# A hybrid attention and gMLP block on one core: the attention's short matmuls issued in two places of a product

## The reference, cut to what matters

```python
h = rms_norm(x, pre_norm)
q, k, v, gate_a, u_b, v_b, gate_b, mg_a, mg_b = split(h @ w_in)
o_a = sliding_window_attention(q, k, v, sinks, rel_bias)   # 16 query heads, 2 kv heads, window 128
y_a = (o_a * silu(gate_a)) @ w_branch_a
o_b = spatial_gating(gelu(u_b), gelu(v_b), ...)
y_b = (o_b * silu(gate_b)) @ w_branch_b
out = (sigmoid(mg_a) * y_a + sigmoid(mg_b) * y_b) @ w_out
x = x + rms_norm(out, post_norm)
```

## Time and profile before

| | |
|---|---|
| median of 3 runs | 908.33 us (908.08 to 909.26) |
| the profiled execution | 907.86 us, its span 906.1 us |
| granted clock of TensorE, mean | 0.998 |
| PE busy | 898.7 us, 99% of the span |
| DVE busy | 640.1 us, 71% |
| ACT busy | 491.0 us, 54% |
| POOL busy | 499.4 us, 55% |

### The profile page before, as it was taken

How to read it: one execution, slowest core, us unless ns; L and a number is a source line. 1 busy time by engine, 2 the same in 40 slices (tenths; PEclk the granted TensorE clock), 3 DMA queues, 4 the chain that set the end, 5 groups by cost and what they waited for, 6 DMA issues and landing times.

```text
span 906.1 us, 12649 instructions
## 1 busy us (share of the span) xinstructions
PE 898.7 (99%) x4332; PEld 754.0 (83%) x4332; DVE 640.1 (71%) x1135; ACT 491.0 (54%) x948; POOL 499.4 (55%) x395
## 2 busy tenths in 40 slices
PE   9999999999999999999999999999999999999997
PEld 7888888888888888888888888888888888888886
DVE  6766794655656564656565678688689878989968
ACT  6554355766756675757566664344444434534563
POOL 4565235777686868695868685445542252043236
PEclk9999999999999999999999999999999999999999
DMA  8889764422222253323222243533188550435004
GB/s 307 195 200 247 243 204 106 136 77 90 71 91 85 82 139 129 94 77 98 72 84 91 82 150 95 187 122 122 59 303 323 186 209 1 139 116 210 1 1 186
DMA packets 126591, 122.50 MB, mean 135 GB/s; under 512 B 23208, under 2 KB 95936, under 8 KB 126272
## 3 DMA queue, kind: packets, MB, share of 16 engines
q1 hardware_dynamic: 124288, 118.27, 41.2%
q10 hardware_dynamic: 2240, 3.43, 1.2%
HBM read 89.68 MB, written 35.15 MB: 138 GB/s over the span
## 4 chain that ended last, share of the span: by engine, by line
PE 98%; ACT 0%; DVE 0%; POOL 0%; issue 0%; DVEq 0%; POOLq 0%; ACTq 0%
PE acc L970 51%; PE acc L1150 11%; PE acc L823 9%; PE ps_m L1150 7%; PE ps_t L1150 7%; PE ps_t L987 3%; PE ps_m L1017 3%; PE acc L913 2%; PE ps_t L997 2%; PE ps_t L853 1%; PE ps_m L853 0%; PE acc L1042 0%; PE ps_t L839 0%; PE ps_t L855 0%; PE ps_m L855 0%
## 5 line engine op out<-in xcount | busy, mean ns | idle before, releaser
L970 PE MATMUL acc<-mv,w_hi 128*128 128x512 f32 x1344 | 353.1, 392 | 0.0
L970 PEld LDWEIGHTS acc<-mv,w_hi 128*128 128x128 f32 x1344 | 245.0, 188 | 45.0
L970 PE MATMUL acc<-mv,w_lo 128*128 128x512 f32 x672 | 181.1, 391 | 0.0
L970 PEld LDWEIGHTS acc<-mv,w_lo 128*128 128x128 f32 x672 | 126.2, 188 | 28.3
L1751 POOL TENSOR_TENSOR w_lo<-sums,w_hi 128x1024 fp32r<-128x1024 f32 x48 | 116.0, 2418 | 46.4 <-ACT w_hi L1316 38.4
L1751 POOL TENSOR_TENSOR w_lo<-raw,w_hi 128x1024 fp32r<-128x1024 f32 (+1 forms) x48 | 95.7, 1994 | 41.5 <-ACT w_hi L1309 35.9
L1150 PE MATMUL acc<-right,left 128*128 128x512 f32 x432 | 98.7, 389 | 0.0
L1150 PEld LDWEIGHTS acc<-right,left 128*128 128x128 f32 x432 | 81.0, 188 | 17.2 <-DVE left L2131 0.4
L1796 POOL TENSOR_SCALAR_AFFINE_SELECT pt_prev<-pt_pack 128x512 fp32r<-128x512 f32 x64 | 41.7, 652 | 85.7 <-DVE pt_pack L2067 85.7
L1518 ACT ACTIVATE prob<-neg_s,neg_max 128x129 f32<-128x129 f32 x128 | 50.6, 397 | 68.6 <-DVE neg_max L2076 68.5
L823 PE MATMUL acc<-mv 128*128 128x512 f32 x288 | 69.3, 394 | 0.6 <-ACT mv L1183 0.6
(11 more groups left out here) (282 smaller groups left out, 1680.8 us busy)
## 6 DMA issues: line engine op xcount, KB each, us to landing
raw<-in_w_in SPq DMA_DIRECT2D x56, 512.0 KB, 4.0
ht_d<-sums SPq DMA_DIRECT2D x8, 512.0 KB, 5.1
mix_d<-mix_b SPq DMA_DIRECT2D x8, 512.0 KB, 3.9
ga_d<-gate SPq DMA_DIRECT2D x16, 256.0 KB, 2.0
tb<-tb_d SPq DMA_DIRECT2D x4, 1024.0 KB, 5.2
ub<-mix_d SPq DMA_DIRECT2D x7, 512.0 KB, 3.5
gb_d<-ub SPq DMA_DIRECT2D x7, 512.0 KB, 2.6
x_both<-in_x SPq DMA_DIRECT2D x6, 512.0 KB, 6.3
```

Source lines behind the costliest of these rows:

```text
L970: ins = nc.tensor.matmul(bank, (w_lo if y == 2 else w_hi)[:, left + k * P:left + (k + 1) * P], right[:, (OPW if y == 1 else 0) + k * HALF: ...
```

## The change

In a product with attention work, transposes and scores come behind the third long matmul, and values behind the ninth. Nothing is added or removed; the order on PE's queue is the only thing that differs, and the other engines' queues are as before.

```diff
-            def attend(p, k):
+            def attend_values(p, k):
                 if 5 <= k < 13:
                     values(p, k - 5)
+
+            def attend_scores(p, k):
                 if 3 <= k < 11:
                     transpose_p(p, k - 3)
                 if k < 8:
...
             def product(n, x, at=None):
                 product_waits(n, x)
                 if at:
-                    product_mms(n, x, 0, 6)
-                    attend(*at)
-                    product_mms(n, x, 6, 12).then_inc(prod, 1)
+                    product_mms(n, x, 0, 3)
+                    attend_scores(*at)
+                    product_mms(n, x, 3, 9)
+                    attend_values(*at)
+                    product_mms(n, x, 9, 12).then_inc(prod, 1)
                 else:
```

## The result

| | before | after |
|---|---|---|
| median | 908.36 us (908.08 to 909.26) | 937.62 us (936.61 to 938.1) |
| span of the profiled execution | 906.1 us | 934.9 us |
| PE busy | 898.7 us, 99% | 907.3 us, 97% |

The ratio is 1.0317, with a 95% interval of 1.0305 to 1.0329: 29.3 us slower, where 25.2 were forecast. The profiled executions lie 28.8 us apart.

A forecast was written before the change was run, and what follows sets the result against it. PE's queue, 99% busy and without waits in the attention, was taken to set the end. Losses of 0.13 + 0.62 + 0.65 + 1.75 = 3.15 us a head pair, times 8 = 25.2, gave a median of 933.5 us, range 919 to 942.

The forecast's parts named there:

- Short matmuls at their usual cost, split at 0: On PE, short matmuls last the same behind short or long ones, so splitting the group in two costs 0.
- the rival "faster": On PE, a second short group behind a long matmul saves 0.05 in 48 steps: 2.4 us, 905.9; chance 0.03.
- Step 5, 0.13: PE's scores in step 5 of a head pair wait for DVE's evaluation of step 4's scores: 0.13 us lost.
- Steps 6 and 7, 0.62 and 0.65: Scores wait for DVE's evaluation, queued behind the pack that waits for values: 0.62 and 0.65 us lost per head pair.
- Step 9, 1.75: Transposes in step 9 wait for step 8's pack, delayed by a chain from step 7's evaluation: 1.75 us per head pair.
- The surcharge of 0.15: Extra cost of the transposes' wait in step 9, taken as the middle between 0.04 and 0.26 us.
- Steps 8 and 10 clear: Transposes in steps 8 and 10 come after the pack they need, with margins of 0.3 us: no loss.
- Eight head pairs alike: Head pair 6 stands for all eight: 3.15 us for a head pair, times 8 = 25.2.
- PE's busy time: In the changed profile, PE's busy time stays within a few microseconds and its idle time grows by 25.
- The rival that put 27 us on the clock: A pause of 1.75 us drops PE from 2.4 to 1.2 GHz for one step: 27 us more, 961; chance 0.03.
- the one in which more follows: POOL's masks and ACT's evictions make a product wait too: up to 1.5 us a pair more, 945; chance 0.06.
- the first rival: Give in the chain hides step 9's loss, only steps 5 to 7 lose: 11.2 us, 919.5; chance 0.10.

The follow-up runs named there:

- experiment 1: Changed kernel with the two groups swapped: values behind the third long matmul, transposes and scores behind the ninth; 909.13 us, ratio to before 1.001.
- experiment 4: Changed kernel with DVE's first two additions of a head pair moved from the end of step 7 to the end of step 8, behind the pack; 922.84 us.
- experiment 8: Changed kernel with values behind the twelfth long matmul, so nine long matmuls between scores and values, not six; 957.75 us, ratio to before 1.053.
- distance 0: Changed kernel with one group behind the sixth long matmul, values last: no long matmuls between scores and values (the distance); 915.23 us, ratio to before 1.0057.
- experiment 3: Changed kernel, PE's order kept, with DVE's evaluation of the scores ahead of the pack of the same step; 909.63 us, ratio to before 1.0021.

## Why the prediction was right

The mechanism, its places and the sign came out as forecast, and the time within 4.1 us. The terms that came out short are small and of one kind, what a signal or a start after a wait costs, but for a delay in one head pair; 0.6 us of the difference stands outside the attention.

*What bounds the kernel.* PE without waits meant that an order can hardly gain. No order tried here is faster than the kernel before, whose order has no wait to remove.

*Short matmuls at their usual cost, split at 0.* Right: experiment 1, which does not show the gain of the rival "faster" either. Transposes and scores still take 0.69 together behind a long matmul, as this row and the next long matmul of the changed kernel show.

```profile
478.03 0.38 PE L997 MATMUL ps_t<-ident,prob 128*128 128x128 f32 x2
...
478.72 1.32 PE L970 MATMUL acc<-mv,w_hi 128*128 128x512 f32 x5
```

The rule weighed against it (the Trainium skill, TensorE: Matmul & The Clock Gate, Back-to-back issue gap, about 81 ns for a 128-column matmul in a stream) does not describe these transposes, at 0.11 in either kernel.

*Step 5, 0.13.* Measured 0.14. The margin of 0.17 less the values' 0.24 was the right reading.

*Steps 6 and 7, 0.62 and 0.65.* Measured 0.74 and 0.72. The term that was mis-sized is the signal from the values to the pack. I took 0.04, the distance from transposes to pack; it is 0.11 (487.52 to 487.63). It applies to both steps. The surcharge of 0.06 on the scores was a little short too: from 489.51 to 489.57 is 0.06, but the second score matmul then follows at 0.22 instead of 0.20.

*Step 9, 1.75.* Measured 1.81. The chain from the evaluation of step 7 to the pack of step 8 is as stiff as assumed, and experiment 4 shows that it is this chain. The surcharge of 0.15 was a middle between two bounds, as no row showed it; by luck it is the distance at which a waiting transpose starts behind the pack (503.13 to 503.28); the second transpose then follows at 0.14 instead of 0.11, which is half of what was short.

*Steps 8 and 10 clear.* Right, with 0.03 and 0.00, and experiment 8 shows how little was left.

*Eight head pairs alike.* Not quite: head pair 4 loses 0.37 more in step 7. The prediction took one head pair for all. In pair 4 the pack of step 6 starts 0.46 behind the values' end instead of 0.11, and the scores of step 7 pay for it. The kernel before already has this pack 0.24 behind the transposes' end instead of 0.04, without loss there. What holds this pack back is open.

*The clock.* The granted clock stayed at 1.00 in the attention part, 2.4 GHz, through eight pauses of 1.6 us and sixteen of 0.5 or less.

```profile
161.00:565.00 404.00, 383.87 (x1945) 317.43 (x1944) 222.11 (x666) 247.01 (x638) 277.38 (x227) 1.00 0.28 88
```

That is the row by stage of 161 to 565 us; the 1.00 is the clock.

*PE's busy time.* This sign was off: it was to stay within a few microseconds and the idle time to grow by 25. Busy time grew by 8.6 and idle time by 20.2 (7.4 to 27.6), since the end of the matmul ahead of each pause, which in a full stream lies under the next matmul, now counts by itself.

The rival that put 27 us on the clock did not come about, nor did the one in which more follows; and the tail of step 9, which the first rival had hidden, was paid in full.

## What to carry to other kernels

Before moving work on the busiest engine, look for waits on its progress on other engines that are met long before they count, and ask what moves them behind their deadline. The price of such a wait is not its length but what stands behind it in its queue: with the same wait of the pack, 28 us became 1.1 us when the evaluation of the scores went ahead of it on DVE. Size it as a margin, from the releaser's end to the need, step by step; here that gave each step within 0.12 us, but for one step of one head pair. Read the margin of every repetition, and take off what a start after a wait costs.

## What the runs showed that was not expected

The loss bends upward with the distance. A head pair loses 0.6 at distance 0, 1.4 at 3, 3.4 at 6 and 6.1 at 9 (sums of the rows above). Once a step waits, it grows by about 0.69 for each three long matmuls, and more steps join as their margins are used up: step 9 waits from distance 0 on, steps 6 and 7 from about 3, steps 8 and 10 from somewhere between 6 and 9. And DVE's product of the gate in step 3 (L2043, 1.60 us in each head pair before) took 0.68 in experiment 3. Before, it starts 0.24 after a POOL operation has begun (L1751); in experiment 3 it starts 0.16 ahead of POOL's mask, and it is the mask that takes 1.02 instead of 0.64. No time hung on it.
